# A third down block and earlier odd gate/up loads in a two-layer hybrid and mixture-of-experts kernel

## The chip, the cores and the metric

The kernel runs on one core of a Trainium2 chip. The metric is device time in microseconds (us) of one execution. Weights lie in HBM and come into SBUF by DMA. The core has a matrix engine (PE), VectorE (DVE), ScalarE (ACT), GpSimd (POOL) and SyncE (SP), which here only issues DMAs and waits for semaphores.

## The reference, cut to what matters

Two layers run over 256 tokens of width 1024, in float32. The second ends in a mixture of experts, and this is the part that the change is about:

```python
h = h + hybrid_mixer(h, ...)          # ... merged @ w_out is its last projection
h = h + hierarchical_moe(h, ...)
# hierarchical_moe: 64 experts, the best 2 for each token
hn = rms_norm_2(h, norm_g)
... # router: p_group, top_w, top_i
yb = (jax.nn.silu(x_blk @ w_gate[e]) * (x_blk @ w_up[e])) @ w_down[e]
out = out.at[slot_tok].add(yb * slot_w[:, None])
```

w_gate and w_up are 1024x256 for each expert, w_down is 256x1024: 3 MB in float32 for one expert, 192 MiB for the 64.

## The kernel before, in words

The program has a front part (projections, attention, the delta rule, o-projection, merge, output projection, router) and then the expert stage. The expert stage is a loop over 16 groups of 4 experts (PER = 4, N_GROUPS = 16). All weights come as blocks of 128 x 4096 float32, which is 2 MiB. A group has four gate/up blocks (one for each expert) and two down blocks (two experts each): 6 blocks, 96 for all groups.

Buffers. gate_up[0] (even groups) is the ring of four 2 MiB slots that the front part also uses: slots 2, 3, 0, 1. gate_up[1] (odd groups) is the list `odd` of four blocks in the arena. `down` has two blocks, which all groups use. The arena holds activations of the front part in the same space, so a block can be loaded only when what stood there has been read.

Work on PE for group n, in the order in which it is written (`step`): gather(n+1) picks the tokens of the next group, turn_over(n) transposes, first_products(n+1) multiplies by the next group's gate/up (L1256, 64 matmuls), second_products(n) multiplies by this group's down (L1273, 32 matmuls), scatter(n) adds to the tokens (L1285). first_products waits for the gate/up blocks of its group, second_products for the down blocks of its own. The last pair of groups is written out: first_products(15) runs k = 0 to 5 (ODD_CUT), then second_products(14), scatter(14), the rest of first_products(15), and second_products(15) in two halves.

What sets the order of loads. All weights are issued by SP on one hardware queue (q1), in program order, and SP waits in between for semaphores. In the front part's end the blocks ZB (z), GD (gate), WD (delta output) and WO2 (output projection), two of each, go through slots 0 and 1 in turn; a block is issued when PE has read the block two before it. When the second WD block has been issued and `o_b` has arrived, SP issues w_router, gate/up block 0 of group 0, and both down blocks of group 0; then the first WO2 block, block 3 of odd group 1, the second WO2 block; then, after `merged2` reaches 4, gate/up block 1 of group 0, and blocks 2 and 3 as slots 0 and 1 come free; after `h2` reaches 9, blocks 0 to 2 of group 1. The even blocks of group 2 follow in parts, after `part_used` and `gate_up` (L2822), and the down blocks of group 1 after `down` reaches 8, which is the end of second_products(0). From then on `refill` goes round:

```python
def refill(g, u):
    sp.wait_ge(sem("gate_up"), g + 2)        # first_products(g - 1) is done
    load_gate_up((g + 1) % N_GROUPS, u)
    sp.wait_ge(sem("down"), 2 * g + 6)       # second_products(g - 1) is done
    load_down(g % N_GROUPS)
```

On PE the o-projection is project_whole of WD and WD + 1, the output projection is project_whole of WO2 (wp0, wp1) and four parts of WO2 + 1; each part is 16 matmuls at L818 (project_part). project_part waits for the block's slot semaphore before its first matmul. DVE merges the branches (L2544, L2545) into y_four, which the output projection reads.

Of the kernel before, what the change touches and what calls it, by code (L numbers as in the profile page):

```python
# [9 lines left out]
SEQ = 256  # L10
P = 128
# [60 lines left out]
def build(nc, A):  # L72
# [3 lines left out]
    with ctx:  # L76
# [207 lines left out]
        rn2_r = rounded(RING + top[0], LEN)  # L284
        top[0] += LEN

        top[0] = solve_at
# [22 lines left out]
        row_of = stat(2 * SUMS - 1)  # L310
        o_rn_r = rounded(RING + zone + 2 * SEQ, SEQ)
        stat_at[0] += -(consts_at + 4 * P + stat_at[0]) % 8
# [38 lines left out]
        w_router = place(KD * 72).rearrange("p (k c) -> p k c", k=KD)  # L351
        rms4 = place(SEQ)
# [4 lines left out]
        r_values = place(TT * 16).rearrange("p (t e) -> p t e", t=TT)  # L357
        chosen = place(TT * 64).rearrange("p (t e) -> p t e", t=TT)
        weight = place(TT * 64).rearrange("p (t e) -> p t e", t=TT)
# [11 lines left out]
        passes_i = place(1)[0:1, :].bitcast(mybir.dt.int32)  # L371

        xg = m_T.rearrange("p k t -> p (k t)")[:, 0:D].rearrange("p (k s) -> p k s", k=KD)
        yb = m_T.rearrange("p k t -> p (k t)")[:, D:2 * D]

        assert top[0] <= ARENA - 6 * BLOCK and zone <= ARENA - 3 * BLOCK, (top[0], zone)
# [3 lines left out]
        odd.append(place(BLOCK))  # L380
        gate_up = [[ring[s] for s in WHOLE_SLOT[-PER:]], odd]
        N_GROUPS = EXPERTS // PER
# [44 lines left out]
        def _(pe):  # L427
# [414 lines left out]
            def meta_level(v):  # L842

                am = mt_am[v]
                if v == 0:
                    pe.wait_ge(sem("m_am"), 1)
# [298 lines left out]
            for j in range(2):  # L1145
                project_whole([f"wd{2 * j}", f"wd{2 * j + 1}"], WD + j, o_T, SEQ, WK, "y_delta")
            project_whole(["wp0", "wp1"], WO2, y_four, SEQ, ready="merged2")
            wp_part = lambda n: project_part(f"wp{n // 2}", WO2 + 1, n // 2 - 2, n % 2, y_four, SEQ)
            wp_part(4)
# [13 lines left out]
            def sums_part(j):  # L1163

                pe.wait_ge(sem("squares"), 13 + j + 1)
                for t, f in enumerate(sums_of):
                    for k in (2 * j, 2 * j + 1):
                        last = nc.tensor.matmul(f.bank[:, 0:1], o_sq[:, k, t * P:(t + 1) * P], ones[:, 0:1],
                                                start=k == 0, stop=k == KD - 1)
                    if j == 3:  # L1170
                        end(f, last)
# [90 lines left out]

            def second_products(n, halves=range(2)):

                pe.wait_ge(sem("hid_T"), n + 1)
                pe.wait_ge(sem("down_in"), 32 * n + 32)
                for half in halves:
                    if half == 1:
                        pe.wait_ge(sem("late_down"), 32 * n + 32)
                    for i in range(2):  # L1270
                        for j in range(PER):
                            c = half * HALF + (j % 2) * D + i * 512
                            last = nc.tensor.matmul(banks[5 + half][j * CAP:(j + 1) * CAP, :], hid_T[:, i, j * CAP:(j + 1) * CAP],  # L1273
                                                    down[j // 2][:, c:c + 512], start=i == 0, stop=i == 1)
                    last.then_inc(sem("down"), 1)
# [12 lines left out]
            def step(n, u):  # L1288

                gather(n + 1, 4 * n + 2)  # L1290
                turn_over(n)
                first_products(n + 1, 1 - u)
                second_products(n)
                scatter(n)

            count = first_count(pe)
            with pe.Fori(0, count) as p:
# [9 lines left out]
                first_products(it + 1, 1, range(ODD_CUT))  # L1307
                second_products(it)
                scatter(it)
# [12 lines left out]

                second_products(it + 1, (0,))
                scatter(it + 1, (0,))
                second_products(it + 1, (1,))
                norm_sums((0,))
# [10 lines left out]
        def _(act):  # L1337
# [239 lines left out]
            lead_for("gsum")  # L1577
            act.wait_ge(sem("gsum"), 1)
            for p, t in regions:
# [5 lines left out]
            def meta_exps():  # L1585
                lead_for("kk_m")
                act.wait_ge(sem("m_u"), 1)
                link(nc.scalar.activation(mt["u"][0:META], mt["u"][0:META], ACT.Exp, scale=-1.0))
                act.sem_inc(sem("m_d"), 1)
# [142 lines left out]
            for j in range(4):  # L1732
                act.wait_ge(sem("h2"), 2 * j + 1)
                nc.scalar.activation(o_sq[:, 2 * j:2 * j + 2, :], res[:, 2 * j:2 * j + 2, META:], ACT.Square).then_inc(sem("squares"), 1)
            nc.scalar.activation(spare[:, 0:1], ones[:, 0:1], ACT.Sqrt)
# [75 lines left out]
        def _(dve):  # L1811
# [425 lines left out]
            dve.sem_inc(free[f.b], 1)  # L2237
            dve.sem_inc(sem("gsum"), 1)

# [28 lines left out]
            def meta_rows():  # L2268
# [6 lines left out]
                dve.sem_inc(free[f.b], 1)  # L2275
                dve.sem_inc(sem("m_u"), 1)

            meta_beta = beta[0:META, 0, 0:HEADS].unsqueeze(2).to_broadcast([META, HEADS, META])

            def meta_a():  # L2280
# [10 lines left out]
                link(last)  # L2291
                dve.sem_inc(sem("m_am"), 1)

# [488 lines left out]
        def _(sp):  # L2782
# [46 lines left out]

            def load_down(q):  # L2830
                for j in range(2):
                    sp.dma_start(down[j], of_group("down", q, j)).then_inc(sem("down_in"), 16)
                sp.sem_inc(sem("late_down"), 32)

            def load_down_half(q, half):

                for j in range(2):
                    c = slice(half * HALF, (half + 1) * HALF)
                    sp.dma_start(down[j][:, c], of_group("down", q, j)[:, c]).then_inc(sem("late_down" if half else "down_in"), 16)
# [33 lines left out]
            sp.wait_ge(sem("down"), 8)  # L2873
            load_down(1)

            def refill(g, u):
# [3 lines left out]
                sp.wait_ge(sem("down"), 2 * g + 6)  # L2880
                load_down(g % N_GROUPS)

# [116 lines left out]
```

## Time and profile before

| what | value |
|---|---|
| median of 3 runs | 1201.8 us (1201.57 to 1202.69) |
| profiled execution, span from first to last instruction | 1201.2 us |
| that execution beside the median | 0.6 us under it |
| PE busy | 1056.9 us (88%) |
| DVE, ACT, POOL busy | 491.7, 356.6, 387.8 us |
| chain that ended last | PE 60%, DMA 27%, DVE 8% |
| DMA | 303.95 MB, mean 253 GB/s |
| queues with data | q1 and q10 hardware_dynamic, q8 and q14 instruction |

The profile is of one execution. Its span is the time to which sums are made. The front part is everything up to about 754 us, where first_products(0) begins; the expert stage is the rest. In the expert stage the DMA moves 428 GB/s in every slice of the page, while PE is busy six to seven tenths. Numbers in front of an engine's row are us from the span's start.

### The profile page before, as it was taken

To read this page: it belongs to the slowest core of one execution; us is meant where nothing else is said; L and a number is where in the kernel's file an instruction comes from. 1 tells how busy PE (TensorE), PEld (TensorE's weight loads), DVE (VectorE), ACT (ScalarE), POOL (GpSimd) and SP (SyncE) were. 2 spreads that over 40 slices of the span, in tenths; PEclk is the share of its full clock that TensorE was granted. 3 is DMA by queue.
4 is the path that set the end of the run, shared out by engine and by line. 5 is a ranking of instruction groups with operands and counts; after the bars stand their busy time and mean duration, and the time that the engine had idled before them with its cause. 6 is when DMAs were issued, how large, how long until landed. Compare 5 with 4: busy or idle time off the path is not lost.

```text
span 1201.2 us, 20207 instructions
## 1 busy us (share of the span) xinstructions
PE 1056.9 (88%) x8237; PEld 852.8 (71%) x8237; DVE 491.7 (41%) x973; ACT 356.6 (30%) x536; POOL 387.8 (32%) x176
## 2 busy tenths in 40 slices
PE   9999999999999999999999998977676676767776
PEld 7999999999999999798989787443333333333334
DVE  4447944701125886667854413221111111111113
ACT  4544253444447557234252103100000000000002
POOL 4867568887877766133030000000000000000000
PEclk8999899999999998999999999998888888888898
DMA  6645446466656444113221685999999999999994
GB/s 232 197 127 157 121 143 201 148 185 185 191 167 205 154 143 140 53 54 140 80 91 43 276 332 213 417 428 428 428 428 428 428 428 429 428 428 428 428 413 178
DMA packets 41552, 303.95 MB, mean 253 GB/s; under 512 B 4869, under 2 KB 5253, under 8 KB 27786
## 3 DMA queue, kind: packets, MB, share of 16 engines
q1 hardware_dynamic: 41194, 302.43, 66.4%
q8 instruction: 51, 0.84, 0.3%
q10 hardware_dynamic: 288, 0.52, 0.1%
q14 instruction: 19, 0.16, 0.0%
HBM read 301.89 MB, written 1.05 MB: 252 GB/s over the span
## 4 chain that ended last, share of the span: by engine, by line
PE 60%; DMA 27%; DVE 8%; issue 1%; ACT 1%; SPq 1%; POOL 1%; DVEq 0%; ACTq 0%; POOLq 0%
DMA arena<-down 20%; PE bank L447 11%; PE bank L448 11%; PE bank L449 11%; PE bank L818 9%; PE bank L1273 4%; DMA weights<-gate_up 4%; PE bank L1256 3%; DMA arena<-gate_up 3%; PE bank L782 1%; DVE arena L1948 1%; PE bank L1227 1%; PE bank L1285 1%; PE bank L1018 1%; PE bank L997 1%
## 5 line engine op out<-in xcount | busy, mean ns | idle before, releaser
L2733 POOL TENSOR_TENSOR rounded<-weights,rounded 128x1024 fp32r<-128x1024 f32 x152 | 368.6, 2452 | 175.7 <-ACT rounded L1350 164.0
L447 PE MATMUL bank<-rounded 128*128 128x256 f32 (+2 forms) x784 | 223.0, 284 | 0.7 <-POOL rounded L2733 0.7
L449 PE MATMUL bank<-rounded 128*128 128x256 f32 (+2 forms) x784 | 221.7, 283 | 0.0
L448 PE MATMUL bank<-rounded 128*128 128x256 f32 (+2 forms) x784 | 221.5, 282 | 0.0
L1350 ACT ACTIVATE rounded<-weights 128x1024 fp32r<-128x1024 f32 x146 | 147.1, 1052 | 85.0 <-PE bank L449 56.0
L447 PEld LDWEIGHTS bank<-rounded 128*128 128x128 f32 (+1 forms) x784 | 147.8, 189 | 2.9 <-POOL rounded L2733 1.2
L448 PEld LDWEIGHTS bank<-rounded 128*128 128x128 f32 (+1 forms) x784 | 147.1, 188 | 0.6 <-issue 0.5
L449 PEld LDWEIGHTS bank<-rounded 128*128 128x128 f32 (+1 forms) x784 | 146.7, 187 | 0.2
L447 PE MATMUL bank<-rounded,rounded 128*128 128x256 f32 (+3 forms) x456 | 131.8, 289 | 2.1 <-DVEq L2178 0.8
L448 PE MATMUL bank<-rounded,rounded 128*128 128x256 f32 (+3 forms) x456 | 130.4, 286 | 0.0
L449 PE MATMUL bank<-rounded,rounded 128*128 128x256 f32 (+3 forms) x456 | 130.2, 286 | 0.0
L818 PE MATMUL bank<-arena,weights 128*128 128x256 f32 x512 | 116.5, 385 | 2.2 <-DVEq L2530 1.6
L1256 PE MATMUL bank<-weights,arena 128*32 128x512 f32 x512 | 67.9, 691 | 47.2 <-DMA weights<-gate_up 45.0
L1256 PE MATMUL bank<-arena 128*32 128x512 f32 x512 | 69.8, 705 | 44.7 <-DMA arena<-gate_up 44.3
L818 PEld LDWEIGHTS bank<-arena,weights 128*128 128x128 f32 x512 | 96.6, 192 | 17.0 <-issue 2.1
L2650 DVE TENSOR_TENSOR arena<-arena,bank 128x256 f32<-128x256 f32 x16 | 6.7, 421 | 204.2 <-ACT arena L1765 204.2
L447 PEld LDWEIGHTS bank<-rounded,rounded 128*128 128x128 f32 (+1 forms) x456 | 86.1, 189 | 4.2 <-issue 1.8
L449 PEld LDWEIGHTS bank<-rounded,rounded 128*128 128x128 f32 (+1 forms) x456 | 85.9, 188 | 0.1
L448 PEld LDWEIGHTS bank<-rounded,rounded 128*128 128x128 f32 (+1 forms) x456 | 85.8, 188 | 0.1
L1256 PEld LDWEIGHTS bank<-weights,arena 128*32 128x32 f32 x512 | 17.6, 126 | 92.1 <-issue 92.1
L1256 PEld LDWEIGHTS bank<-arena 128*32 128x32 f32 x512 | 17.3, 127 | 91.2 <-DMA arena<-gate_up 46.0
L1285 PE MATMUL bank<-arena 128*128 128x256 f32 x256 | 59.7, 386 | 14.1 <-DVE arena L2655 13.3
(444 smaller groups left out, 1348.5 us busy)
## 6 DMA issues: line engine op xcount, KB each, us to landing
weights<-front SPq DMA_DIRECT2D x152, 512.0 KB, 4.3
arena<-down SPq DMA_DIRECT2D x30, 2048.0 KB, 20.6
weights<-gate_up SPq DMA_DIRECT2D x28, 2048.0 KB, 33.4
arena<-gate_up SPq DMA_DIRECT2D x28, 2048.0 KB, 33.2
weights<-front SPq DMA_DIRECT2D x8, 2048.0 KB, 8.3
arena<-gate_up SPq DMA_DIRECT2D x4, 1536.0 KB, 32.9
weights<-gate_up SPq DMA_DIRECT2D x4, 1024.0 KB, 15.3
arena<-down SPq DMA_DIRECT2D x4, 1024.0 KB, 8.0
```

The lines of the kernel that those rows point to most:

```text
L447: nc.tensor.matmul(out, a[0], b[1], start=start, stop=False)
L448: nc.tensor.matmul(out, a[0], b[0], start=False, stop=False)
L449: return nc.tensor.matmul(out, a[1], b[0], start=False, stop=stop)
L782: last = nc.tensor.matmul(f.bank[0:SUMS, 0:n], row_of[:, SUMS - 1 - c:2 * SUMS - 1 - c], squares[:, h, 0:n], start=h == 0, stop=h == HEADS ...
L818: last = nc.tensor.matmul(f.bank[:, j * n:(j + 1) * n], w[:, c:c + P], x[:, k, :], start=k == 0, stop=k == KD - 1)
L997: last = nc.tensor.matmul(f.bank[:, i * P:(i + 1) * P], system[:, l.s + i, :], x, start=True, stop=True)
L1018: last = nc.tensor.matmul(o, new_v[l.n][:, i, :], qk[:, l.s + i, :], start=not has_state, stop=True)
L1256: last = nc.tensor.matmul(banks[3][j * CAP:(j + 1) * CAP, :], xg[:, k, j * CAP:(j + 1) * CAP], gate_up[u][j][:, k * 2 * FE:(k + 1) * 2 * F ...
L1273: last = nc.tensor.matmul(banks[5 + half][j * CAP:(j + 1) * CAP, :], hid_T[:, i, j * CAP:(j + 1) * CAP], down[j // 2][:, c:c + 512], start ...
L1285: last = nc.tensor.matmul(banks[b][:, j * SEQ:(j + 1) * SEQ], yb[:, c:c + P], pick_T, start=True, stop=True)
L1350: nc.scalar.activation(w_hi[h % SPLIT][:, quarter(q)], raw[q % RAW], ACT.Copy).then_inc(sem("w_hi"), 1)
L2733: nc.gpsimd.tensor_tensor(lo, raw[q % RAW], hi.bitcast(f32), ALU.subtract).then_inc(sem("w_lo"), 1)
```

## The change

Three things change. The build asks for a dynamic DMA scratch of 1024 bytes for each partition, and the arena grows by 3840 columns. In that space a third down block down_c stands: a group's first down block goes to down_a in even groups and to down_c in odd groups, and its second to down_b in all. And the loads are issued in another order. The first down block of group 1 is issued before the first GD block. Odd gate/up blocks 2 and 3 of group 1 are issued right after the down blocks of group 0, ahead of the first WO2 block; odd blocks 0 and 1 after gate/up block 1 of group 0. The merged activations are written to y_sum (the space of m_tok), o_rn_r and the squares of h move too, so that the odd blocks' space is free at those points. Some semaphores are joined (gsum into gl, m_u and m_am into m_rows).

```diff
-        RING, ARENA = SLOTS * BLOCK, 36824
+        RING, ARENA = SLOTS * BLOCK, 40664
...
+        y_sum = m_tok.rearrange("p t c -> p (t c)").rearrange("p (k t) -> p k t", k=KD)
+        h_sq = arena[:, r_values_end:r_values_end + KD * SEQ].rearrange("p (k t) -> p k t", k=KD)
...
-        top[0] = ARENA - 6 * BLOCK
+        top[0] = ARENA - 7 * BLOCK
         odd = [place(BLOCK) for _ in range(3)]
-        down = [place(BLOCK) for _ in range(2)]
+        down_a, down_b = (place(BLOCK) for _ in range(2))
         odd.append(place(BLOCK))
+        down_c = place(BLOCK)
+        down = [[down_a, down_b], [down_c, down_b]]
...
-            def second_products(n, halves=range(2)):
+            def second_products(n, u, halves=range(2)):
                 pe.wait_ge(sem("hid_T"), n + 1)
-                pe.wait_ge(sem("down_in"), 32 * n + 32)
+                if u == 0:
+                    pe.wait_ge(sem("down_a_in"), 8 * n + 16)
+                else:
+                    pe.wait_ge(sem("down_c_in"), 8 * n + 8)
+                pe.wait_ge(sem("down_b_in"), 16 * n + 16)
...
-                link(nc.vector.tensor_tensor(y4, y4, g_g[:, j], ALU.add))
+                link(nc.vector.tensor_tensor(y_sum[:, 2 * j:2 * j + 2, :], y4, g_g[:, j], ALU.add))
...
-            def load_down(q):
-                for j in range(2):
-                    sp.dma_start(down[j], of_group("down", q, j)).then_inc(sem("down_in"), 16)
-                sp.sem_inc(sem("late_down"), 32)
+            def load_down_first(q, u):
+                sp.dma_start(down[u][0], of_group("down", q, 0)).then_inc(sem("down_c_in" if u else "down_a_in"), 16)
+            def load_down_second(q):
+                sp.dma_start(down_b, of_group("down", q, 1)).then_inc(sem("down_b_in"), 16)
+                sp.sem_inc(sem("late_down"), 16)
...
+                if ZB + i == GD:
+                    load_down_first(1, 1)
                 if ZB + i == WO2:
                     sp.wait_ge(sem("o_b"), 4)
                     sp.dma_start(w_router, A["w_router"]).then_inc(sem("router_in"), 16)
                     load_gate_up(0, 0, [0])
-                    load_down(0)
-                if ZB + i == WO2 + 1:
-                    load_gate_up(1, 1, [3])
+                    load_down_first(0, 0)
+                    load_down_second(0)
+                    load_gate_up(1, 1, [2, 3])
...
             sp.wait_ge(sem("merged2"), 4)
             load_gate_up(0, 0, [1])
+            load_gate_up(1, 1, [0, 1])
...
-            sp.wait_ge(sem("h2"), 9)
-            load_gate_up(1, 1, range(3))
...
             sp.wait_ge(sem("down"), 8)
-            load_down(1)
+            load_down_second(1)
+            load_down_first(2, 0)
...
                 sp.wait_ge(sem("down"), 2 * g + 6)
-                load_down(g % N_GROUPS)
+                load_down_second(g % N_GROUPS)
+                load_down_first((g + 1) % N_GROUPS, u)
...
             sp.wait_ge(sem("down"), 2 * n_groups + 2)
-            load_down(N_GROUPS - 2)
+            load_down_second(N_GROUPS - 2)
             load_odd_part(N_GROUPS - 1, ODD_CUT, KD)
+            load_down_first(N_GROUPS - 1, 1)
...
-    nc = bacc.Bacc("TRN2", target_bir_lowering=False, num_devices=1)
+    nc = bacc.Bacc("TRN2", target_bir_lowering=False, num_devices=1, dynamic_dma_scratch_size=1024)
```

PE, DVE, ACT and POOL issue the same instructions in the same order as before; the order of SP's issues changes at these places. First SP before the change, from the second WD block (bank1_full) to the first part of group 2; "weights<-front" are the WD and WO2 blocks, "weights<-gate_up" even and "arena<-gate_up" odd blocks.

```order
L2857 DMA weights<-front 128x4096 [waits bank1_full]
L2849 DMA arena<-w_router 128x576 [waits o_b]
L2814 DMA weights<-gate_up 128x4096
L2832 DMA arena<-down 128x4096 x2
L2857 DMA weights<-front 128x4096 [waits bank7_full]
L2814 DMA arena<-gate_up 128x4096
L2857 DMA weights<-front 128x4096 [waits bank4_full]
L2814 DMA weights<-gate_up 128x4096 [waits merged2]
L2814 DMA weights<-gate_up 128x4096 [waits bank0_full]
L2814 DMA weights<-gate_up 128x4096 [waits bank2_full]
L2814 DMA arena<-gate_up 128x4096 [waits h2]
L2814 DMA arena<-gate_up 128x4096 x2
```

The same stretch of SP after the change.

```order
L2874 DMA weights<-front 128x4096 [waits bank1_full]
L2866 DMA arena<-w_router 128x576 [waits o_b]
L2826 DMA weights<-gate_up 128x4096
L2844 DMA arena<-down 128x4096
L2848 DMA arena<-down 128x4096
L2826 DMA arena<-gate_up 128x4096 x2
L2874 DMA weights<-front 128x4096 [waits bank7_full]
L2874 DMA weights<-front 128x4096 [waits bank4_full]
L2826 DMA weights<-gate_up 128x4096 [waits merged2]
L2826 DMA arena<-gate_up 128x4096 x2
L2826 DMA weights<-gate_up 128x4096 [waits bank0_full]
L2826 DMA weights<-gate_up 128x4096 [waits bank2_full]
```

Two odd blocks now stand between the down blocks and the first WO2 block (the row with bank7_full), one that stood behind it is gone, and the wait for h2 is gone.

The second place is SP's end: the six blocks' worth of loads after the loop, before the change.

```order
L2828 DMA arena<-gate_up 128x3072 [waits gate_up]
L2828 DMA arena<-gate_up 128x3072 x3
L2890 ISA
L2832 DMA arena<-down 128x4096 [waits down]
L2832 DMA arena<-down 128x4096
L2828 DMA arena<-gate_up 128x1024 x4
L2894 REGISTER_ALU
L2839 DMA arena<-down 128x2048 [waits down]
L2839 DMA arena<-down 128x2048
```

And after it.

```order
L2840 DMA arena<-gate_up 128x3072 [waits gate_up]
L2840 DMA arena<-gate_up 128x3072 x3
L2907 ISA
L2848 DMA arena<-down 128x4096 [waits down]
L2840 DMA arena<-gate_up 128x1024 x4
L2844 DMA arena<-down 128x4096
L2912 REGISTER_ALU
L2854 DMA arena<-down 128x2048 [waits down]
```

Between the three quarters of group 15's gate/up (128x3072) and its rest (128x1024) one down block is issued where there were two; the first down block of group 15 follows the rest whole, and only the second comes in halves.

## Rows read from the trace of the kernel before

**Rows 1.** The page's head and its chain that ended last, by engine.

```profile
span 1201.2 us, 20207 instructions
...
PE 60%; DMA 27%; DVE 8%; issue 1%; ACT 1%; SPq 1%; POOL 1%; DVEq 0%; ACTq 0%; POOLq 0%
```

**Rows 2.** Stretches: busy us of each engine, granted clock, DMA share, GB/s.

```profile
560.00:570.00 10.00, 10.00 (x52) 7.17 (x52) 5.08 (x13) 4.25 (x6) 0.00 (x0) 1.00 0.00 0
...
680.00:700.00 20.00, 20.00 (x94) 17.65 (x93) 4.16 (x6) 0.00 (x0) 0.00 (x0) 1.00 1.01 427
...
779.00:1157.80 378.80, 269.13 (x1967) 139.56 (x1965) 79.55 (x163) 26.47 (x54) 0.00 (x0) 0.88 1.01 428
```

**Rows 3.** SP in order of time, 669 to 705: start, us, what it issued.

```profile
669.58 0.33 SPq L2857 DMA_DIRECT2D weights<-front  x1
...
670.43 0.44 SPq L2814 DMA_DIRECT2D weights<-gate_up  x1
670.99 1.07 SPq L2832 DMA_DIRECT2D arena<-down  x2
688.79 0.33 SPq L2857 DMA_DIRECT2D weights<-front  x1
689.16 0.43 SPq L2814 DMA_DIRECT2D arena<-gate_up  x1
```

**Rows 4.** DMAs issued at 669.58, 670.43, 670.99, 688.79, 689.16, 775.90: us to landing last.

```profile
weights<-front SPq DMA_DIRECT2D x1, 2048.0 KB, 8.1
...
weights<-gate_up SPq DMA_DIRECT2D x1, 2048.0 KB, 13.8
...
arena<-down SPq DMA_DIRECT2D x1, 2048.0 KB, 18.1
...
weights<-front SPq DMA_DIRECT2D x1, 2048.0 KB, 10.1
...
arena<-gate_up SPq DMA_DIRECT2D x1, 2048.0 KB, 14.6
...
arena<-down SPq DMA_DIRECT2D x1, 2048.0 KB, 9.4
```

**Rows 5.** PE and DVE in order of time, o-projection: start, us, instructions.

```profile
677.27 42.57 PE L818 MATMUL bank<-arena,weights 128*128 128x256 f32 x196 [0.54 <-DVEq L2530]
...
702.61 0.69 DVE L2544 TENSOR_TENSOR weights<-bank,weights 128x512 f32<-128x512 f32 x1 [5.49 <-PE bank L818]
```

**Rows 6.** SP in order of time, at the first groups.

```profile
754.75 7.76 SPq L2822 DMA_DIRECT2D weights<-gate_up  x12
775.90 0.80 SPq L2832 DMA_DIRECT2D arena<-down  x2
777.99 2.09 SPq L2814 DMA_DIRECT2D arena<-gate_up  x4
```

**Rows 7.** PE in order of time, three first_products; idle before each in brackets.

```profile
785.27 7.07 PE L1256 MATMUL bank<-weights,arena 128*32 128x512 f32 x64 [0.82 <-DVE arena L2640]
...
809.88 9.92 PE L1256 MATMUL bank<-arena 128*32 128x512 f32 x64 [5.49 <-DMA arena<-gate_up]
...
1045.08 8.38 PE L1256 MATMUL bank<-arena 128*32 128x512 f32 x64 [7.28 <-DMA arena<-gate_up]
```

**Rows 8.** Stretches with a lower clock, columns as in rows 2.

```profile
809.80:820.00 10.20, 10.12 (x68) 2.50 (x72) 0.00 (x0) 0.05 (x1) 0.00 (x0) 0.71 1.00 427
...
1167.70:1172.80 5.10, 5.07 (x32) 1.16 (x32) 0.00 (x0) 0.60 (x1) 0.00 (x0) 0.71 0.82 280
```

**Rows 9.** PE in order of time, the last groups.

```profile
1143.17 3.64 PE L1273 MATMUL bank<-arena 128*32 128x512 f32 x32 [1.15 <-DMA arena<-down]
...
1157.88 5.36 PE L1256 MATMUL bank<-arena 128*32 128x512 f32 x48 [2.46 <-DMA arena<-gate_up]
1167.70 5.07 PE L1273 MATMUL bank<-arena 128*32 128x512 f32 x32 [4.46 <-DMA arena<-down]
...
1181.41 1.92 PE L1273 MATMUL bank<-arena 128*32 128x512 f32 x16 [0.47 <-ACT arena L1770]
```

More of the change, by code:

```diff
@@ L285, in build @@
         top[0] += LEN
+        free_from = top[0]
         top[0] = solve_at
@@ L351, in build @@
         w_router = place(KD * 72).rearrange("p (k c) -> p k c", k=KD)
-        rms4 = place(SEQ)
+        o_rn_r = rounded(RING + top[0], SEQ)
+        top[0] += SEQ
         router = place(TT * 72).rearrange("p (t c) -> p t c", t=TT)
@@ L357, in build @@
         r_values = place(TT * 16).rearrange("p (t e) -> p t e", t=TT)
+        r_values_end = top[0]
         chosen = place(TT * 64).rearrange("p (t e) -> p t e", t=TT)
@@ L371, in build @@
         passes_i = place(1)[0:1, :].bitcast(mybir.dt.int32)
+        y_sum = m_tok.rearrange("p t c -> p (t c)").rearrange("p (k t) -> p k t", k=KD)
+        assert r_values_end + KD * SEQ <= top[0] - 1
+        h_sq = arena[:, r_values_end:r_values_end + KD * SEQ].rearrange("p (k t) -> p k t", k=KD)
         xg = m_T.rearrange("p k t -> p (k t)")[:, 0:D].rearrange("p (k s) -> p k s", k=KD)
         yb = m_T.rearrange("p k t -> p (k t)")[:, D:2 * D]
-        assert top[0] <= ARENA - 6 * BLOCK and zone <= ARENA - 3 * BLOCK, (top[0], zone)
-        top[0] = ARENA - 6 * BLOCK
+        assert top[0] <= ARENA - 7 * BLOCK, top[0]
+        top[0] = ARENA - 7 * BLOCK
         odd = [place(BLOCK) for _ in range(3)]
-        down = [place(BLOCK) for _ in range(2)]
+        down_a, down_b = (place(BLOCK) for _ in range(2))
         odd.append(place(BLOCK))
+        assert top[0] >= free_from, (top[0], free_from)
+        down_c = place(BLOCK)
+        down = [[down_a, down_b], [down_c, down_b]]
         gate_up = [[ring[s] for s in WHOLE_SLOT[-PER:]], odd]
@@ L845, in meta_level @@
                 if v == 0:
-                    pe.wait_ge(sem("m_am"), 1)
+                    pe.wait_ge(sem("m_rows"), 2)
                 else:
@@ L1146, in _ @@
                 project_whole([f"wd{2 * j}", f"wd{2 * j + 1}"], WD + j, o_T, SEQ, WK, "y_delta")
-            project_whole(["wp0", "wp1"], WO2, y_four, SEQ, ready="merged2")
-            wp_part = lambda n: project_part(f"wp{n // 2}", WO2 + 1, n // 2 - 2, n % 2, y_four, SEQ)
+            project_whole(["wp0", "wp1"], WO2, y_sum, SEQ, ready="merged2")
+            wp_part = lambda n: project_part(f"wp{n // 2}", WO2 + 1, n // 2 - 2, n % 2, y_sum, SEQ)
             wp_part(4)
@@ L1167, in sums_part @@
                     for k in (2 * j, 2 * j + 1):
-                        last = nc.tensor.matmul(f.bank[:, 0:1], o_sq[:, k, t * P:(t + 1) * P], ones[:, 0:1],
+                        last = nc.tensor.matmul(f.bank[:, 0:1], h_sq[:, k, t * P:(t + 1) * P], ones[:, 0:1],
                                                 start=k == 0, stop=k == KD - 1)
@@ L1273, in second_products @@
                             last = nc.tensor.matmul(banks[5 + half][j * CAP:(j + 1) * CAP, :], hid_T[:, i, j * CAP:(j + 1) * CAP],
-                                                    down[j // 2][:, c:c + 512], start=i == 0, stop=i == 1)
+                                                    down[u][j // 2][:, c:c + 512], start=i == 0, stop=i == 1)
                     last.then_inc(sem("down"), 1)
@@ L1292, in step @@
                 first_products(n + 1, 1 - u)
-                second_products(n)
+                second_products(n, u)
                 scatter(n)
@@ L1307, in _ @@
                 first_products(it + 1, 1, range(ODD_CUT))
-                second_products(it)
+                second_products(it, 0)
                 scatter(it)
@@ L1321, in norm_sums @@
                     return last
-                second_products(it + 1, (0,))
+                second_products(it + 1, 1, (0,))
                 scatter(it + 1, (0,))
-                second_products(it + 1, (1,))
+                second_products(it + 1, 1, (1,))
                 norm_sums((0,))
@@ L1577, in _ @@
             lead_for("gsum")
-            act.wait_ge(sem("gsum"), 1)
+            act.wait_ge(sem("gl"), 3)
             for p, t in regions:
@@ L1586, in meta_exps @@
                 lead_for("kk_m")
-                act.wait_ge(sem("m_u"), 1)
+                act.wait_ge(sem("m_rows"), 1)
                 link(nc.scalar.activation(mt["u"][0:META], mt["u"][0:META], ACT.Exp, scale=-1.0))
@@ L1733, in _ @@
                 act.wait_ge(sem("h2"), 2 * j + 1)
-                nc.scalar.activation(o_sq[:, 2 * j:2 * j + 2, :], res[:, 2 * j:2 * j + 2, META:], ACT.Square).then_inc(sem("squares"), 1)
+                nc.scalar.activation(h_sq[:, 2 * j:2 * j + 2, :], res[:, 2 * j:2 * j + 2, META:], ACT.Square).then_inc(sem("squares"), 1)
             nc.scalar.activation(spare[:, 0:1], ones[:, 0:1], ACT.Sqrt)
@@ L2237, in _ @@
             dve.sem_inc(free[f.b], 1)
-            dve.sem_inc(sem("gsum"), 1)
+            dve.sem_inc(sem("gl"), 1)
             def fold(g):
@@ L2275, in meta_rows @@
                 dve.sem_inc(free[f.b], 1)
-                dve.sem_inc(sem("m_u"), 1)
+                dve.sem_inc(sem("m_rows"), 1)
             meta_beta = beta[0:META, 0, 0:HEADS].unsqueeze(2).to_broadcast([META, HEADS, META])
@@ L2291, in meta_a @@
                 link(last)
-                dve.sem_inc(sem("m_am"), 1)
+                dve.sem_inc(sem("m_rows"), 1)
             def meta_t(v):
@@ L2828, in load_odd_part @@
                     sp.dma_start(gate_up[1][j][:, c], of_group("gate_up", q, j)[:, c]).then_inc(sem("late_odd" if a else "odd_in"), 16)
-            def load_down(q):
-                for j in range(2):
-                    sp.dma_start(down[j], of_group("down", q, j)).then_inc(sem("down_in"), 16)
-                sp.sem_inc(sem("late_down"), 32)
+            def load_down_first(q, u):
[3 more added lines that the diff above has]
+                sp.sem_inc(sem("late_down"), 16)
             def load_down_half(q, half):
-                for j in range(2):
-                    c = slice(half * HALF, (half + 1) * HALF)
-                    sp.dma_start(down[j][:, c], of_group("down", q, j)[:, c]).then_inc(sem("late_down" if half else "down_in"), 16)
+                c = slice(half * HALF, (half + 1) * HALF)
+                sp.dma_start(down_b[:, c], of_group("down", q, 1)[:, c]).then_inc(sem("late_down" if half else "down_b_in"), 16)
             sp.wait_ge(sem("w_lo"), 2 * N_HALVES)
```

3 lines of the change are left out of this document (1 added, 2 removed).

## Prediction

> **What bounds the kernel now.** I read the page's head and chain first [rows 1]: 60% of the last chain is PE, 27% DMA, so there are two regimes. The stretches tell them apart. Until SP's first part for group 2 at 754.75 [rows 6] PE sets the pace; from 779 to 1157.8 the DMA runs at 428 GB/s with share 1.01 while PE is busy 269 of 379 us [rows 2]. A 2 MiB block at 428 GB/s is 4.9 us. Then I read SP's issues with their landings [rows 3, 4], since one queue feeds everything, and last PE's waits at the first and last groups [rows 5 to 9].
>
> The landings behind the o-projection say how the queue behaves. Issue plus time to landing gives 677.7 (second WD block), 684.2 (gate/up 0, with w_router's 288 KB before it), 689.1 (down, first), then, one block skipped, 698.9 (first WO2 block, issued at 688.79) and 703.8 (odd block 3) [rows 3, 4]. Each is 4.9 us behind the one ahead: the blocks are moved one after the other in the order of issue. The DMA is full from 680 to 700 [rows 2].
>
> **The change part by part.**
>
> Scratch, arena, joined semaphores, moved buffers: nothing. They change addresses, and every engine but SP issues the same instructions. Data moves on hardware queues alone, so no row shows a user of the scratch; I take 0. From the rows a bound is only that a block's 4.9 us and a matmul's time stay what they are.
>
> First down block of group 1 before GD: it is issued right behind the second z block, SP's next step there is a wait for PE, and soon after the DMA is idle, with share 0.00 from 560 to 570 [rows 2]. It costs 0 and takes one block (4.9 us) out of what the full queue has to move later. What that is worth is worked out at the end of the stream.
>
> Odd blocks 2 and 3 ahead of WO2. In the changed order of SP they follow the down blocks at about 672 us, and the first WO2 block is issued at 688.79 as before, since that issue waits for PE's end with the first WD block, which is not touched. But the queue ahead of it is two blocks longer: down second 694.0, odd 2 at 698.9, odd 3 at 703.8, WO2 at 708.7. PE is through with the WD blocks at 702.6: DVE begins on the last of their products at 702.61, released by PE [rows 5]. Before, WO2 had been there since 698.9, and PE ran 196 matmuls in 42.57 us with no gap [rows 5]. Now PE waits 708.7 - 702.5 = 6.2 us. Queued behind that wait on PE are all of the output projection, the router and the gather; DVE's and ACT's norm and routing wait for those. I find no work on any engine that could fill it, so it goes 1 to 1 to first_products(0).
>
> Clock after that wait. In the expert stage a PE that sat idle 5.49 us took 9.92 us for 64 matmuls that take 7.07 us warm, and after 7.28 us idle 8.38 [rows 7]; the clock granted in 809.8 to 820 was 0.71, a mix of 1.2 and 2.4 GHz [rows 8]. So a wait of 6.2 us costs 1.3 to 2.9 us more; I take 2.0, the mean over the nine such groups from 809.88 to 1045.08, whose first and smallest are shown. Together the front part ends 8.2 us later (7.5 to 9.1).
>
> Odd blocks 0 to 3 of group 1 loaded before first_products(0). They save no time by themselves. Before, three of these and group 2's even blocks kept the queue full until past 775.90; now the queue is empty when group 2's parts are issued, at 754.75 plus the delay. Those are 4 blocks, 19.6 us, and if they begin to move 1.8 us after the issue (an estimate: not less than the 1.3 that the two landings below differ by, not more than 8.1 less 4.9), they are through at 776.2 plus the delay, in time for second_products(0)'s end at 775.9 [rows 6] and the same 1.8 us. There SP issues two down blocks, then four odd ones, in both kernels. The first down block landed after 9.4 us because the queue still had work; behind an empty queue a block lands after 8.1 us [rows 4]. So from here on the stream is 1.3 us earlier: -1.3.
>
> So all buffers are full at this point in both kernels, and the only lasting gain is the one extra block, group 1's first down block. From 775.9 to the landing of the first three quarters of group 15's gate/up both kernels move 77 blocks (before: 96 less 14 loaded, less down 14, the rest of 15 and down 15, 5 in all; after: 96 less 15, less 4). That landing is at 1157.8 before [rows 9] and 1157.8 - 1.3 + 8.2 = 1164.7 after. In the loop SP issues the next load 3.7 us after a down block has landed, when four blocks (19.6 us) are still queued, so the stream doesn't break.
>
> The end. Before, first_products(15) ran 5.36 us from 1157.88, PE then stood 4.46 us for down 14, and second_products(14) took 5.07 us at clock 0.71 where it takes 3.64 warm [rows 8, 9]. That is 14.9 us. After, one down block is left to come instead of two: it lands 4.9 us after the quarters, PE is busy for 5.36 of that, and second_products(14) follows with no idle and so, I take it, warm: 5.36 + 3.64 = 9.0. Gain 5.9 us; if it stays at the lower clock, 4.5.
> Then the rest of 15, its first down block and the first half of the second must land before second_products(15): quarters + 4.9 x 3 + 2.4 = 17.1 us. PE comes there at 5.4 + (1181.41 - 1167.70) - 1.4 = 17.7 us. Just in time, so nothing is lost.
>
> Sum: + 6.2 + 2.0 - 1.3 - 5.9 = + 1.0 us. On the profiled span that is 1202.2; that execution lay 0.6 under the median, so 1202.8 us is forecast.
>
> **A rule weighed.** The rows show landings in issue order, 4.9 us apart [rows 3, 4]. The Trainium skill, DMA: Bandwidth & Descriptors, section "Queues, rings and completion order", says that descriptors are consumed in ring order on each DMA engine but that completion isn't first-in first-out for an issuing engine. By its first half PE waits, as summed; by its second a WO2 block might land ahead of the odd blocks, which would be the first rival below. The landings of this trace side with the first half.
>
> **The rivals.**
>
> A. No wait at WO2, because the queue mixes or reorders the blocks. For it: nothing in the trace; against it: the equal steps of 4.9 us. Then the delay and the clock's price fall away: -1.3 - 5.9 = -7.2, 1194.6 us. If the wait is only half as long (3 us, no loss of clock), 3 - 7.2 = -4.2 us, 1197.6.
>
> B. The clock takes more, and the kernel is slower. The mechanism is the lower clock after the wait at WO2: 2.9 us lost there as after 809.88, and second_products(14) at the lower clock as before, so 4.5 gained at the end. + 6.2 + 2.9 - 1.3 - 4.5 = + 3.3: 1205.1 us. It decides from the point where clock losses together exceed the forecast's by 1.4 us. For it: idle of 5.5 to 7.5 us was followed by a loss every time. Against it: the size varied between 1.3 and 2.9, and before, the second product at the end lost time only after its own 4.46 us of idle.
>
> C. The third block buys nothing at the end, because the last loads come so late that second_products(15) waits for them, or the stream breaks at a down wait. Then + 8.2 - 1.3 = + 6.9: 1208.7 us. Against it: the margins of 16 us in the loop and 0.6 at the end.
>
> **How the numbers follow.** The forecast (a wait of about 6 us that nearly pays for the gain) has 0.50, B 0.25, A and its half form 0.18, C 0.07. The measurement can tell about 0.2%, which is 2.4 us: 1199.4 to 1204.2 counts as no change. The forecast's own range is 1201 to 1204.3: the clock term runs from 1.3 to 2.9, the router's stretch, which starts and stops PE, may shift by a microsecond. Faster comes from A and a little of the forecast's lower end (0.19), slower from B, C and the upper end (0.33), the rest is same (0.48). The range 1196.5 to 1206.0 takes in B and the half form of A and leaves out full A and C.
>
> **What would show it.** In the changed trace: the first WO2 block lands 19.9 us after its issue (10.1 before), and PE has one idle stretch of 6.2 us between 702.5 and 708.7 released by a DMA to weights; matmuls at L818 after it at a lower clock for some microseconds; the first part for group 2 is issued at 762 to 764 (754.75 before); the first down block issued after second_products(0) lands after about 8.1 us; the DMA rate is 428 GB/s to the end; the idle before second_products(14) is gone, and it takes 3.6 us. The forecast is wrong if WO2 lands in issue order but PE's wait is under 4 us, if anything in the loop waits longer than before, or if the loss of clock appears at a place where before had none.

## The result and the profile after

The changed kernel took 1205.49 us (median of 7, 1203.89 to 1208.27); the kernel before 1201.20 (median of 7 by then). The ratio is 1.0033, 95% interval 1.0018 to 1.0048. A second measurement, of twelve runs, gave 1.0025 [1.0009, 1.0040]; from here on the brackets behind a ratio are its 95% interval. So the kernel is slower by 3 to 4 us. The forecast was 1202.8 us, in the range 1196.5 to 1206.0.

First the head and the last chain of the changed kernel's page, which answer to [rows 1].

```profile
span 1203.2 us, 20223 instructions
...
PE 61%; DMA 26%; DVE 8%; issue 2%; SPq 1%; ACT 1%; POOL 1%; DVEq 0%; ACTq 0%; POOLq 0%
```

SP in order of time at the o-projection (start, us, what), for [rows 3], and then the landing of the first WO2 block, for [rows 4].

```profile
668.27 0.33 SPq L2874 DMA_DIRECT2D weights<-front  x1
...
669.67 0.53 SPq L2844 DMA_DIRECT2D arena<-down  x1
670.24 0.46 SPq L2848 DMA_DIRECT2D arena<-down  x1
670.81 0.90 SPq L2826 DMA_DIRECT2D arena<-gate_up  x2
687.47 14.14 SPq L2874 DMA_DIRECT2D weights<-front  x2
```

```profile
weights<-front SPq DMA_DIRECT2D x1, 2048.0 KB, 19.8
```

Issued at 687.47, landed at 707.3: 19.8 us where it was 10.1. PE in order of time shows who paid, the answer to [rows 5]; in brackets the idle time before and what ended it.

```profile
707.33 20.55 PE L826 MATMUL bank<-arena,weights 128*128 128x256 f32 x80 [6.08 <-DMA weights<-front]
...
754.93 3.83 PE L1235 MATMUL bank<-arena 128*128 128x128 f32 x32 [1.70 <-DVE arena L2635]
```

PE stands 6.08 us, and the 80 matmuls behind it take 20.55 us; at the rate before, 196 in 42.57 us, they take 17.4. (The profile counts each of these float32 matmuls twice: a part that the kernel writes as 8 has 16 records, and first_products, which is written as 32, has 64. All counts here are the profile's.) The stretches (busy us by engine, granted clock, DMA share, GB/s) show the clock that goes with it: still 0.95 in the wait, 0.50 right after it, that is 1.2 GHz.

```profile
701.20:707.30 6.10, 0.05 (x1) 0.00 (x0) 1.38 (x2) 0.00 (x0) 0.00 (x0) 0.95 1.01 430
707.30:711.00 3.70, 3.67 (x9) 2.95 (x10) 0.00 (x0) 0.00 (x0) 0.00 (x0) 0.50 1.02 434
...
764.00:767.00 3.00, 3.00 (x32) 0.74 (x24) 0.00 (x0) 0.00 (x0) 0.00 (x0) 1.00 0.96 264
...
784.00:1164.40 380.40, 268.61 (x1974) 140.00 (x1972) 80.47 (x164) 26.46 (x54) 0.00 (x0) 0.86 1.01 428
```

The last of these rows answers to the long one of [rows 2]: the same 428 GB/s to the end. The row at 764 to 767 is the queue after it has run empty, when group 2's small first parts start it again. SP at the first groups, for [rows 6]:

```profile
761.17 8.14 SPq L2834 DMA_DIRECT2D weights<-gate_up  x12
782.32 0.33 SPq L2848 DMA_DIRECT2D arena<-down  x1
782.75 0.36 SPq L2844 DMA_DIRECT2D arena<-down  x1
784.35 2.09 SPq L2826 DMA_DIRECT2D arena<-gate_up  x4
```

And PE where group 3, group 14 and then group 15 land, for [rows 7, 9].

```profile
816.57 8.39 PE L1264 MATMUL bank<-arena 128*32 128x512 f32 x64 [5.77 <-DMA arena<-gate_up]
...
1140.12 8.75 PE L1264 MATMUL bank<-weights,arena 128*32 128x512 f32 x64 [7.64 <-DMA weights<-gate_up]
1148.69 3.61 PE L1285 MATMUL bank<-arena 128*32 128x512 f32 x32
...
1164.53 6.78 PE L1264 MATMUL bank<-arena 128*32 128x512 f32 x48 [3.60 <-DMA arena<-gate_up]
1171.13 3.61 PE L1285 MATMUL bank<-arena 128*32 128x512 f32 x32
...
1183.55 1.92 PE L1285 MATMUL bank<-arena 128*32 128x512 f32 x16 [0.65 <-ACT arena L1782]
```

The 4.46 us of idle before second_products(14) is gone, and it takes 3.61 us instead of 5.07. But first_products(15) in front of it takes 6.78 instead of 5.36.

Four stretches, each from one event to the next in one trace, make every kernel below comparable. A: from the issue of the second WD block to group 2's first part. B: from there to the start of first_products(3), which waits for its blocks. C: on to the start of first_products(15). D: on to the end of the span.

| trace | A | B | C | D | span |
|---|---|---|---|---|---|
| before | 85.17 | 55.13 | 348.00 | 43.32 | 1201.2 |
| changed | 92.90 | 55.40 | 347.96 | 38.67 | 1203.2 |
| changed, again | 93.14 | 56.05 | 347.96 | 40.58 | 1204.0 |

The second WD block is issued at 669.58 before, at 668.27 and 666.27 in the changed kernel's two traces: what lies ahead of the change varies by more than 3 us between executions of the kernels in this study (666.2 to 669.8 in the eleven traces), which is as much as the effect. The stretches take this out. In the first pair of traces A costs 7.73 us, B 0.27, D gives back 4.65: + 3.3 us. With the second trace of the changed kernel the same sum is + 7.97 + 0.92 - 2.74 = + 6.1 us, so single traces scatter by some 3 us inside the stretches too, and the size of the effect is taken from the ratios.

### The profile page after: what moved, and what is told of

It is laid out like the page before. It is cut to its first block, busy times and chain, and to the rows that moved or that the text cites. A ratio compares the mean times of both kernels' runs of the same rounds, so it can differ in the third digit from the quotient of the medians.

```text
span 1203.2 us, 20223 instructions
## 1 busy us (share of the span) xinstructions
PE 1054.7 (88%) x8237; PEld 850.5 (71%) x8237; DVE 491.9 (41%) x973; ACT 356.5 (30%) x536; POOL 387.9 (32%) x176
## 4 chain that ended last, share of the span: by engine, by line
PE 61%; DMA 26%; DVE 8%; issue 2%; SPq 1%; ACT 1%; POOL 1%; DVEq 0%; ACTq 0%; POOLq 0%
DMA arena<-gate_up 23%; PE bank L455 11%; PE bank L456 11%; PE bank L457 11%; PE bank L826 8%; PE bank L1264 6%; PE bank L1285 3%; DMA weights<-front 2%; PE bank L790 1%; DVE arena L1960 1%; SPq L2826 1%; PE bank L1235 1%; PE bank L1297 1%; PE bank L1026 1%; PE bank L1005 1%
## 5 line engine op out<-in xcount | busy, mean ns | idle before, releaser
L826 PE MATMUL bank<-arena,weights 128*128 128x256 f32 x512 | 119.8, 392 | 8.3 <-DMA weights<-front 6.1
L1777 ACT ACTIVATE arena<-bank 128x256 f32<-128x256 f32 x16 | 6.1, 383 | 224.8 <-PE bank L1264 224.8
```

The costliest lines, as they stand in the source:

```text
L826: last = nc.tensor.matmul(f.bank[:, j * n:(j + 1) * n], w[:, c:c + P], x[:, k, :], start=k == 0, stop=k == KD - 1)
```

## The experiments

Ratios are to the kernel before, run on the same chip. Each experiment had 5 rounds, the last one 3. Below each expectation stands what was measured.

**e0_after_again.** No edit.

> The changed kernel again, as the neighbour of the next three. Every theory: 1.002 to 1.005 of the kernel before (about 1205.5 against 1201.2 us), PE idle 6.1 us ahead of the first WO2 block, that block landing about 20 us after its issue. If the span's first 668 us are again 1.3 us shorter than in the first profile of the kernel before, that shift is not an effect of one run.

1206.18 us, 1.0025 [1.0009, 1.0040], idle at WO2 6.16 us. The 1.3 us by which the part ahead of the change was shorter proved to be the spread of executions: here it was 3.3.

**e1_wo2_first.**

```diff
-                    load_gate_up(1, 1, [2, 3])         # under ZB + i == WO2
+                if ZB + i == WO2 + 1:
+                    load_gate_up(1, 1, [2, 3])
```

> The changed kernel with odd blocks 2 and 3 issued behind the first WO2 block instead of ahead of it; all else, the third down block too, stays. Queue theory (the two blocks ahead of WO2 make PE wait): WO2 lands 10 us after its issue, PE has no wait at it, the front part ends 7.7 us earlier than in the changed kernel (6.1 of wait and the clock loss behind it), and nothing is lost later: 1205.5 - 7.7 = 1197.8 us, ratio to the kernel before 0.997. Rival (the loss lies in layout, scratch or the third block): no change from 1205.5, ratio 1.003.

1198.35 us, 0.9969 [0.9954, 0.9984]. The ratio is 0.0056 under the changed kernel's on the same chip, which is 6.7 us (the medians differ by 7.8), for two blocks moved behind one. WO2 landed 10.2 us after its issue, and PE in its trace runs through, 124 matmuls from the window's start on with no wait:

```profile
689.64 26.93 PE L826 MATMUL bank<-arena,weights 128*128 128x256 f32 x124
```

```profile
weights<-front SPq DMA_DIRECT2D x1, 2048.0 KB, 10.2
```

The queue theory holds. The rival falls: scratch, layout and third block are all still in.

**e6_one_ahead.** Odd block 3 ahead of WO2, block 2 behind it.

> The changed kernel with one odd block (3) ahead of WO2 and the other (2) behind it. Queue theory: WO2 lands 4.9 us earlier than in the changed kernel, about 15 us after its issue, PE waits 6.1 - 4.9 = 1.2 us, too short for a loss of clock behind it, so 1.2 us of the 7.7 remain: 1198.4 + 1.2 = 1199.6 us, ratio 0.998. Rival (any wait there costs the clock too): 1.2 + 3.2 us, 1202.8. If blocks don't queue one behind the other: half of the wait, 3 us.

1198.81 us, 0.9969 [0.9958, 0.9980]. WO2 landed 15.1 us after its issue: 10.2, 15.1 and 19.8 us for none, one and two blocks ahead. The landing, PE's row, and the stretch that begins with it (granted clock 1.00):

```profile
weights<-front SPq DMA_DIRECT2D x1, 2048.0 KB, 15.1
```

```profile
704.14 17.53 PE L826 MATMUL bank<-arena,weights 128*128 128x256 f32 x80 [1.36 <-DMA weights<-front]
```

```profile
704.10:708.00 3.90, 3.86 (x18) 3.42 (x19) 0.13 (x1) 0.00 (x0) 0.00 (x0) 1.00 1.00 424
```

A wait of 1.36 us and no loss of clock: 17.53 us for the 80 matmuls. In the totals this kernel can't be told from e1. The rival with a clock loss after any wait falls for a wait of this length.

**e5_kept_warm.** The changed kernel with four matmuls of 128x512, whose results nobody reads, put on PE ahead of the wait (x8 in the profile).

```diff
+            keep_busy("busy2", 4)
             project_whole(["wp0", "wp1"], WO2, y_sum, SEQ, ready="merged2")
```

> The changed kernel with four matmuls of 128x512 (0.9 us each) that compute nothing put on PE just ahead of its wait for the first WO2 block, so that PE is busy during most of that wait. The wait's end does not move. Clock theory: the 80 matmuls behind the wait take 17.4 us instead of 20.6, so 3.2 us less, of which up to 1.7 may be lost again at gather(0), which was slow before and fast in the changed kernel: 1202.3 to 1204 us. If the clock plays no part: 1205.5, unchanged.

1203.67 us, 1.0011 [0.9995, 1.0026]. The total alone doesn't decide it, since the intervals of this and of the changed kernel overlap. The trace does (PE in order of time, then the stretch behind the wait):

```profile
703.77 3.70 PE L1153 MATMUL bank<-arena 128*128 128x512 f32 x8 [1.56 <-DVEq L2560]
708.65 17.53 PE L826 MATMUL bank<-arena,weights 128*128 128x256 f32 x80 [1.18 <-DMA weights<-front]
```

```profile
708.60:712.00 3.40, 3.35 (x16) 2.96 (x17) 0.00 (x0) 0.00 (x0) 0.00 (x0) 1.00 0.99 419
```

The 80 matmuls take 17.53 us again instead of 20.55 or 18.93, and the clock behind the wait is 1.00 where it was 0.50. A is 90.25 us, 2.7 to 2.9 less than in the changed kernel; beside its second trace 1.6 us of that is gather(0), which was slow there and fast here. So of A's 7.7 to 8.0 the wait is 6.1 and the rest is what the clock cost, on balance.

**e2_layout.** The kernel before with `ARENA = 40664` (tiles keep their places) and `dynamic_dma_scratch_size=1024`.

> The kernel before with only the dynamic-transfer scratch of 1024 and the longer arena (all tiles keep their places in it; the 3840 new columns stay empty). No load moves. My theory: no effect, ratio 1.000, 1202 us. Rival (scratch size or the arena's new addresses slow DMA or engines): part of the 1.003 of the changed kernel appears here.

1202.37 us, 1.0002 [0.9989, 1.0015]. A 85.18, B 55.56, D 43.36. Scratch and a longer arena cost nothing that these runs can tell (the interval allows 0.15% at most).

**e3_no_third.** The changed kernel with two down blocks, loaded as before; the odd blocks stay ahead of WO2.

```diff
-        down = [[down_a, down_b], [down_c, down_b]]
+        down = [[down_a, down_b], [down_a, down_b]]
...
-                if ZB + i == GD:
-                    load_down_first(1, 1)
...
-                load_down_second(g % N_GROUPS)
-                load_down_first((g + 1) % N_GROUPS, u)
+                load_down_first(g % N_GROUPS, 1 - u)
+                load_down_second(g % N_GROUPS)
```

> The changed kernel without the third down block: group 1's first down block is not loaded before GD, all groups use down_a and down_b, and down loads stand where the kernel before has them; odd blocks 2 and 3 still go ahead of WO2. Theory: the wait at WO2 stays (PE idle 6.1 us) and the gain at the end is gone (4.4 us between the landing of group 15's first three quarters and the end, 43.3 instead of 38.9 us): 1206 + 4.4 = 1210.5 us, ratio 1.007. Rival (the third block brings nothing, the gain lies in the moved loads): 1206, ratio 1.003.

1208.63 us, 1.0054 [1.0040, 1.0069]; 1.007 was expected and lies just outside. D is 44.63 us. The waits at the end are those of before, but second_products(14) takes 6.36 us behind the second one where it took 5.07:

```profile
1165.27 5.36 PE L1264 MATMUL bank<-arena 128*32 128x512 f32 x48 [2.48 <-DMA arena<-gate_up]
1175.13 6.36 PE L1285 MATMUL bank<-arena 128*32 128x512 f32 x32 [4.50 <-DMA arena<-down]
```

**e4_odd_early_only.** Both edits: no third block, odd blocks 2 and 3 behind WO2. What is left is that group 1's odd blocks come before first_products(0).

> Both removed: no third down block, and odd blocks 2 and 3 behind the first WO2 block; what is left of the change is that all four odd blocks of group 1 are loaded before first_products(0). Theory: nothing gained or lost, 1202 to 1203 us, ratio 1.000 to 1.001 (the buffers are full at the end of second_products(0) either way, and an emptied queue costs up to 1.2 us). Rival (early odd loads gain by themselves): ratio 0.997 or less.

1202.78 us, 1.0005 [0.9993, 1.0017]. The early odd loads gain nothing by themselves. With e1 (0.9969) this prices the third block at 0.0036, 4.3 us. Other pairs give other prices: e3 beside the changed kernel's two ratios 2.5 to 3.5 us, e7 (below) beside the kernel before 5.0 us. Each of these ratios has an interval of about 0.0015 to either side, so the block is worth 2.5 to 5 us, and not better known.

**e7_third_only.** The third block alone; the odd blocks where they were.

```diff
-            load_gate_up(1, 1, [0, 1])
...
+            sp.wait_ge(sem("h2"), 9)
+            load_gate_up(1, 1, range(3))
```

> The changed kernel with the odd gate/up blocks of group 1 where the kernel before loads them (block 3 behind the first WO2 block, blocks 0 to 2 after the wait for h2); only the third down block is left of the new order. Theory that the early odd loads save nothing: the same time as with all four early behind WO2, 1196.5 to 1198 us, because all buffers are full at the end of second_products(0) either way. Rival that the early odd blocks bring part of the gain (they spare up to 1.3 us of queue): 1198 to 1199.5, slower than e1_wo2_first.

1197.84 us, 0.9958 [0.9943, 0.9973], the same as e1 within the intervals; A 85.17, B 55.72, D 38.58. PE at the end:

```profile
1156.52 6.72 PE L1264 MATMUL bank<-arena 128*32 128x512 f32 x48 [3.66 <-DMA arena<-gate_up]
1163.06 3.61 PE L1285 MATMUL bank<-arena 128*32 128x512 f32 x32
```

**e8_wide_first.** As e1, with group 2's first part k = 0 and 1.

```diff
-                    if u == 0 and k in (0, KD // 2 - 1):
+                    if u == 0 and k in (1, KD // 2 - 1):
...
-            load_even_part(2, 0, 1)
+            load_even_part(2, 0, 2)
-            load_even_part(2, 1, KD // 2)
+            load_even_part(2, 2, KD // 2)
```

> As e1_wo2_first, but group 2's even blocks come first in a part of k = 0 and 1 (512 KB for each expert, rows of 4 KB) once first_products(0) has done k = 1, then k = 2 and 3, instead of k = 0 alone (256 KB, rows of 2 KB), then k = 1 to 3. In the changed kernel the DMA moved 264 GB/s in the 3 us in which the 256 KB parts ran behind an empty queue, and the 1.3 us that the emptied queue was to give did not come. Theory that short rows are what slowed it: 400 GB/s or more in the 3 us that begin 2.8 us after the first issue; that issue comes 0.9 us later; group 3's blocks land 55 to 55.6 us behind where the first issue stood before (56.3 in e1), and the kernel is at most 1 us faster, 1197.5 to 1198.5. Rival (the queue's start or SP's issue rate slows it, whatever the rows): the rate stays below 330 GB/s and the landing moves out by 0.9 us.

1196.35 us, 0.9958 [0.9939, 0.9978]. The DMA moved 369 GB/s in the 3 us that begin 2.8 us after the first issue, against 262 in e1 (first e8, then e1):

```profile
754.80:757.80 3.00, 3.00 (x31) 1.28 (x24) 0.00 (x0) 0.60 (x1) 0.00 (x0) 1.00 0.99 369
```

```profile
752.60:755.60 3.00, 3.00 (x32) 0.81 (x24) 0.00 (x0) 0.00 (x0) 0.00 (x0) 1.00 0.93 262
```

The rate is less than the 400 expected, but more than the rival allows, and the kernel came out faster than the 1197.5 to 1198.5 us expected. In the total e8, e7 and e1 are not apart. first_products(3) starts 55.1 us behind the point where e1's order would have issued the first part (751.12, which is 1.12 us into first_products(0)), against 56.33 in e1. That does not show that short rows were the cause, for two reasons. First, in e4, which has the short first part and the empty queue too, B is 54.61 us, less than e8's 55.1. Second, the next part of each block has rows of 6 KB, and it ran no faster. By the size of the packets, 83% of the bytes that e1 moved in the 2 us from 754.86, and 91% in the changed kernel's from 766.17, came in rows of 6 KB (first e1, then the changed kernel):

```profile
754.86:756.86 2.00, 2.00 (x22) 1.16 (x15) 0.00 (x0) 0.92 (x1) 0.00 (x0) 1.00 0.92 244
```

```profile
766.17:768.17 2.00, 2.00 (x22) 1.16 (x15) 0.00 (x0) 0.92 (x1) 0.00 (x0) 1.00 0.85 232
```

e8 changed the length of the rows and the size of the first part together, so what made its queue fuller stays open.

**All traces side by side.** A to D as above; gather(0) is the time of the 32 matmuls just ahead of first_products(0); then the time of first_products(14), PE's idle before first_products(15), and the time of its first 48 matmuls. All in us. For e8, A and B have the later issue of its first part in them (0.87 us); 83.5 and 55.1 are comparable.

| trace | A | B | C | D | gather(0) | fp(14) | idle | fp(15) |
|---|---|---|---|---|---|---|---|---|
| before | 85.17 | 55.13 | 348.00 | 43.32 | 5.46 | 8.56 | 2.46 | 5.36 |
| e2 | 85.18 | 55.56 | 347.95 | 43.36 | 5.46 | 8.75 | 2.45 | 5.36 |
| changed | 92.90 | 55.40 | 347.96 | 38.67 | 3.83 | 8.75 | 3.60 | 6.78 |
| e0 | 93.14 | 56.05 | 347.96 | 40.58 | 5.46 | 8.49 | 3.86 | 8.21 |
| e1 | 83.54 | 56.33 | 347.89 | 37.82 | 3.83 | 10.00 | 2.34 | 5.36 |
| e6 | 85.18 | 57.33 | 347.93 | 39.67 | 3.83 | 9.05 | 3.29 | 7.05 |
| e5 | 90.25 | 55.94 | 348.00 | 39.38 | 3.83 | 9.40 | 2.96 | 7.05 |
| e3 | 92.58 | 55.85 | 347.94 | 44.63 | 3.83 | 9.84 | 2.48 | 5.36 |
| e4 | 83.54 | 54.61 | 347.96 | 43.60 | 3.83 | 9.07 | 2.54 | 7.05 |
| e7 | 85.17 | 55.72 | 347.95 | 38.58 | 5.46 | 8.69 | 3.66 | 6.72 |
| e8 | 84.40 | 54.25 | 347.97 | 38.79 | 3.83 | 8.92 | 3.43 | 6.95 |

## Why the prediction was right where it was, and where it missed

**The wait at WO2** was the step on which the forecast turned, and it held almost to the digit: a landing of 19.9 us after issue was forecast, 19.8 measured; a wait of 6.2, 6.08 and 6.16 measured. e1 and e6 show the cause, since each block moved behind WO2 takes 4.7 to 4.9 us off the landing. One reading on the way was off: the prediction has every landing 4.9 us behind the one ahead, but from the second WD block (677.7) to gate/up 0 (684.2) it is 6.5 us, of which w_router's 288 KB are 0.7 at 428 GB/s. The steps that the forecast used, from 684.2 on, are 4.9.

**The clock after it**, taken at 2.0 (1.3 to 2.9): 3.2 us on the 80 matmuls in the first trace, of which 1.6 came back, as gather(0) took 3.83 us instead of 5.46; 1.5 us in the second trace, where gather(0) stayed at 5.46. A less the wait is 1.7 and 1.8 us. e5 shows it to be the clock. But that the size came out near 2.0 was luck: the loss on the 80 matmuls in the first trace is over the range's upper end of 2.9, and what brought it back was gather(0), of which the prediction says nothing. Beside e1, whose gather(0) was fast too, the changed kernel's A is 9.4 us longer, 6.1 of wait and about 3.2 of clock. gather(0) took 3.83 or 5.46 us in the eleven traces, and no run shows what decides it.

**Scratch, layout, semaphores at 0**: right (e2). **Odd blocks early at 0**: right (e4, and e7 beside e1). **The stream doesn't break**: right, C is 348.0 us in both.

**The emptied queue**, - 1.3: wrong. Stretch B is 55.40 and 56.05, not 53.8. The prediction had the four even blocks of group 2 through in 19.6 us at 428 GB/s. The first parts ran at 264, and the first down block landed 9.7 us after its issue (9.4 before, 8.1 forecast). The term that was mis-sized measured + 0.3 to + 0.9. Over all traces B is 54.6 to 57.3 us with the queue emptied (e8, with its larger first part, left out) and 55.1 to 55.7 with it full (before, e2, e7), so there is no gain to be seen. What slows the queue in those microseconds stays open (see e8).

**The end**, - 5.9 with second_products(14) warm, that is at full clock, - 4.5 otherwise: 4.65 and 2.74 measured. PE's idle before second_products(14) went and the product got shorter, as forecast. What the prediction missed is the product ahead of it. It took first_products(15) at 5.36 us from before, where it followed 2.46 us of idle. In the loop before, second_products(13) still waited 1.15 us for its down blocks [rows 9]; now it doesn't, and this wait moved to the next one, 2.46 + 1.15 = 3.6. After 3.60, 3.66 and 3.86 us of idle (the changed kernel, e7, e0) the 48 matmuls took 6.78, 6.72 and 8.21; after 3.29 and 2.96 (e6, e5) 7.05, after 3.43 (e8) 6.95. In e1, with 2.34 us, they took 5.36. The kernels with two down blocks, e3 and e4, had 2.48 and 2.54 us of idle and took 5.36 and 7.05. The idle itself depends on the clock one group earlier: group 15's blocks come 24.4 us after group 14's in every trace, so the time of first_products(14), the idle, and second_products(13)'s wait where there is one add up to 12.2 to 12.4 us in all eleven. e1's idle was short because its first_products(14) took 10.00 us. So the clock loss changed its place rather than going away. By the prediction's own signs this part was wrong: a loss of clock appeared where before had none, and PE's idle at products in the loop grew (9.12 us before the product at 846.14, 7.50 before the same one at 839.44), though the loop as a whole didn't (C).

**From the span to the median**, + 0.6: wrong. The prediction read the execution with the span 1201.2 as one of the runs at 1201.8. In the ten executions profiled after it, device time is 1.9 to 2.5 us over the span (1205.49 and 1203.2, 1206.23 and 1204.0, 1203.03 and 1200.7, 1212.27 and 1209.9), so the one profiled before was about 1203.5 (an estimate from these differences), one to two us over its kernel's median. The misreading doesn't touch the forecast: 1201.2 + 1.0 + 0.6 is the median of 1201.8 plus the sum's + 1.0. What brought the forecast nearer to 1205.5 was chance, since that median of three lay 0.6 us over the 1201.20 that seven runs gave.

**The sum**: + 1.0 forecast; + 3.3 and + 6.1 by the two traces of the changed kernel; + 4.0 and + 3.0 by the ratios of the two measurements (0.33% and 0.25% of 1202). Rival B had named this size (+ 3.3) and this mechanism, the lower clock, though at the other of the two products. Rival A (no wait) and C (no gain at the end) are out: e6 for A, e3 against the changed kernel for C. The forecast's most likely case was "no change", and it should have been "slower": the 1.3 us of the emptied queue and 1.2 to 3.2 us of the gain at the end did not come.

Left open: why the stretch ahead of the change varies from 666.2 to 669.8 us; why gather(0) is fast in some executions; what slows the loads behind an emptied queue; and what decides whether a short idle costs the clock, since 2.48 us cost nothing in e3 and 2.54 us cost 1.7 us in e4.

## What to carry to other kernels

A prefetch issued ahead of a transfer that an engine will soon wait for, on a queue that serves in order, delays that transfer by the prefetch's whole length, and the engine waits for what goes beyond the slack: ask of each new issue what stands behind it and when that is due. Here WO2 had landed 3.7 us before PE came to it; one block ahead of it (4.9 us) cost a wait of 1.4 us, two cost 6.1 and the clock on top. The same two loads issued after that transfer turned 1.0025 into 0.9969. When loads bound a stage, only what is resident at the moment when all buffers are full counts; loading the same blocks earlier was worth nothing here (e4), and one more buffer is worth at most about its block (4.9 us, less what the engine then does slower). And a wait that goes from one instruction turns up at the next, in one piece, where it may be long enough to cost the clock.

## What the runs showed of the hardware that was not expected

When the queue had run empty, it did not come back to 428 GB/s at once. With first parts of 256 KB for each block the DMA moved 262 to 264 GB/s in the 3 us from 2.8 us after the first issue, and 232 to 244 in the 2 us after 5 us, when most bytes came in rows of 6 KB; at 9 to 14 us after the issue e1 was back at 428. With first parts of 512 KB (e8) it moved 369 in the same 3 us. Behind a queue with work in it the same small parts cost next to nothing: between the issue and group 3 the kernel before took 55.13 us, no longer than the 55.1 of e8.

The clock's price is not fixed. In twelve groups of the loop before, after 5.5 to 7.5 us of idle, 64 matmuls took 8.38 to 9.92 us where 7.07 is warm, and after 6.08 and 6.16 us of idle the 80 matmuls behind WO2 lost 3.2 and 1.5 us. Four matmuls whose results nobody reads, in the middle of that idle time, kept the clock at 1.00 (e5).
